# The folding product of the wide gates moved between the two tiles of the first ups block, the second activation ahead of the next rounded block

## What is computed

```python
def moe_swiglu(h, w_router, w_gu, w_down):
    logits = (h @ w_router).astype(jnp.float32)
    top_vals, top_idx = lax.top_k(logits, TOP_K)
    gates = jax.nn.softmax(top_vals, axis=-1)
    comb = jnp.sum(jax.nn.one_hot(top_idx, N_EXPERTS, dtype=jnp.float32) * gates[..., None],
                   axis=-2).astype(h.dtype)
    y = jnp.zeros_like(h)
    for e in range(N_EXPERTS):
        y = y + comb[..., e:e + 1] * swiglu(h, w_gu[e], w_down[e])
    return y
```

## Time and profile before

| | |
|---|---|
| median of 3 runs | 1629.64 us (1624.52 to 1630.21) |
| profiled execution, its own time | 1629.51 us |
| span from first to last instruction in it | 1627.7 us |
| PE, PEld, DVE, ACT busy | 1555.3, 1269.9, 1243.3, 1030.2 us |
| expert stage with the side expert | about 1000 to 1615 us of the span |
| wide chunks | 7, the folding product of the first at 1038.7 us, of the last at 1531.9 us |

### The profile page before, as it was taken

The page is one execution under the profiler, slowest core; times in us unless marked ns, Lnnn a source line. Parts: engine busy times, 40 slices in busy tenths (PEclk is TensorE's granted clock), DMA queues, the critical chain, the costliest instruction groups (busy, mean ns, idle before and its releaser), DMA issues.

```text
span 1627.7 us, 21967 instructions
## 1 busy us (share of the span) xinstructions
PE 1555.3 (96%) x7408; PEld 1269.9 (78%) x7409; DVE 1243.3 (76%) x1079; ACT 1030.2 (63%) x926; POOL 108.0 (7%) x87
## 2 busy tenths in 40 slices
PE   8999999999999898999999999999999999999997
PEld 6887778888789776677887887777777877787775
DVE  6744655544459878998888888887978797879788
ACT  5344444434345647887777768676768676867675
POOL 0000000000000005304003001000020002000000
PEclk9999999999989999999999999999999999999999
DMA  9663555555543037999998998999899989998994
GB/s 343 222 202 107 169 167 189 199 183 195 177 144 104 27 104 256 393 395 362 380 371 303 375 374 297 353 350 359 299 361 351 384 292 361 354 387 284 362 326 192
DMA packets 195751, 449.75 MB, mean 276 GB/s; under 512 B 8629, under 2 KB 17373, under 8 KB 195678
## 3 DMA queue, kind: packets, MB, share of 16 engines
q1 hardware_dynamic: 193340, 444.84, 76.0%
q10 hardware_dynamic: 2338, 3.88, 0.7%
HBM read 447.64 MB, written 1.05 MB: 276 GB/s over the span
## 4 chain that ended last, share of the span: by engine, by line
PE 69%; DVE 16%; issue 6%; DMA 4%; ACT 3%; DVEq 1%; ACTq 0%; POOL 0%; POOLq 0%; SPq 0%
PE bank L1717 14%; PE bank L1710 10%; PE bank L1711 10%; DVE wlo L985 9%; PE bank L1799 6%; DMA raw<-in_moe_w_down 4%; DVE y L1256 4%; PE bank L1788 3%; PE bank L1952 3%; PE bank L1740 3%; PE bank L1741 2%; PE bank L1747 2%; PE bank L1790 2%; PE bank L1791 2%; ACT whi L512 2%
## 5 line engine op out<-in xcount | busy, mean ns | idle before, releaser
L985 DVE TENSOR_TENSOR wlo<-raw,whi 128x2048 fp32r<-128x2048 f32 x422 | 956.2, 2290 | 238.8 <-ACT whi L512 235.8
L512 ACT ACTIVATE whi<-raw 128x2048 fp32r<-128x2048 f32 x422 | 804.1, 1917 | 395.1 <-PE bank L1717 240.4
L1717 PE MATMUL bank<-wlo,xx 128*128 128x512 f32 x1200 | 335.0, 401 | 29.6 <-DVE wlo L985 27.6
L1717 PEld LDWEIGHTS bank<-wlo,xx 128*128 128x128 f32 x1200 | 220.0, 189 | 107.3 <-DVE wlo L985 64.7
L1710 PE MATMUL bank<-whi,xx 128*128 128x512 f32 x648 | 255.0, 393 | 3.9 <-DVE xx L1464 2.3
L1711 PE MATMUL bank<-whi,xx 128*128 128x512 f32 x648 | 252.9, 390 | 0.0
L1708 PE MATMUL bank<-whi,xx 128*128 128x512 f32 x552 | 153.9, 401 | 0.4 <-ACT whi L512 0.2
L1710 PEld LDWEIGHTS bank<-whi,xx 128*128 128x128 f32 x648 | 121.9, 188 | 30.3 <-issue 3.5
L1711 PEld LDWEIGHTS bank<-whi,xx 128*128 128x128 f32 x648 | 122.0, 188 | 24.8
L1799 PE MATMUL bank<-wlo,hT 128*128 128x512 f32 x504 | 136.0, 392 | 1.3 <-DVE wlo L985 1.3
L1708 PEld LDWEIGHTS bank<-whi,xx 128*128 128x128 f32 x552 | 102.1, 190 | 23.2 <-issue 1.8
(11 more groups left out here) (294 smaller groups left out, 1696.7 us busy)
## 6 DMA issues: line engine op xcount, KB each, us to landing
raw<-in_moe_w_gu SPq DMA_DIRECT2D x224, 1024.0 KB, 7.7
raw<-in_moe_w_down SPq DMA_DIRECT2D x112, 1024.0 KB, 7.7
raw<-in_ffn_w_gu SPq DMA_DIRECT2D x28, 1024.0 KB, 5.1
raw<-in_ret_w_in SPq DMA_DIRECT2D x24, 1024.0 KB, 7.4
raw<-in_ffn_w_down SPq DMA_DIRECT2D x14, 1024.0 KB, 5.0
raw<-in_ret_w_out SPq DMA_DIRECT2D x8, 1024.0 KB, 5.0
raw<-in_conv_w_pw SPq DMA_DIRECT2D x16, 512.0 KB, 4.5
raw<-in_conv_w_pw SPq DMA_DIRECT2D x4, 1024.0 KB, 4.9
```

The costliest lines, as they stand in the source:

```text
L512: nc.scalar.activation(whi[base % SPLIT][:, :], raw[base % RAW][:, :], ACT.Copy).then_inc(hi_done, 1)
L985: nc.vector.tensor_tensor(wlo[base % SPLIT][:, :], raw[base % RAW][:, :], whi[base % SPLIT][:, :].bitcast(f32), ALU.subtract).then_inc(lo_ ...
L1717: last = nc.tensor.matmul(dst[:, :], both, wl, start=False, stop=closing and kc == DC - 1)
```

## The change

Two instructions change places on ACT, and one group on PE. On PE the wait for `gate1_out`, its branch and the folding product come ahead of the products of tile 2 in the first ups block, and so ahead of the `pe_done` of that block. On ACT the second silu comes ahead of hi(block). No instruction is added or taken away.

```diff
                 nc.scalar.activation(sgate[:, 1, :], bank[1][:, :], ACT.Copy).then_inc(gate1_out, 1)
                 nc.scalar.activation(sgate[:, 0, :], bank[0][:, :], ACT.Silu)
-                hi(block, six)
                 act.wait_ge(gate1_ps, count)
                 nc.scalar.activation(sgate[:, 1, :], bank[1][:, :], ACT.Silu).then_inc(silu_done, 2)
+                hi(block, six)
```

```diff
                     with pe.Else():
                         block_columns(base + 2 + half, bank[3], half, 3, HALF_FULL, six)
-                    block_columns(base + 2 + half, bank[2], half, 2, FULL, six).then_inc(pe_done, 1)
                     if half == 0:
                         pe.wait_ge(gate1_out, free)
                         with pe.If(need > 2):
                             nc.tensor.matmul(bank[1][:, :], ident, sgate[:, 1, :], start=True, stop=True).then_inc(gate1_ps, 1)
                         with pe.Else():
                             nc.tensor.matmul(bank[1][:, :], fold, sgate[:, 1, :], start=True, stop=True).then_inc(gate1_ps, 1)
+                    block_columns(base + 2 + half, bank[2], half, 2, FULL, six).then_inc(pe_done, 1)
```

## The result

The changed kernel takes 1633.6 us (median of 11 runs, 1631.62 to 1635.99). The kernel before, beside it, takes 1627.13 us (11 runs, 1622.22 to 1630.21). The ratio is 1.0048, with a 95% interval of 1.0039 to 1.0057: it is slower by 7.8 us, between 6.3 and 9.3. The ratio and its interval come from the single runs; it isn't the ratio of the two medians, which are 6.5 us (0.40%) apart.

The account below looks back on a forecast made before the run. The prediction took PE to bound the wide chunks: 1629.51 us plus seven stalls of 1.3 us gives 1638.6, and with the median 0.13 us above that execution 1638.7 us, 0.56% slower; range 1631 to 1643 us.

Parts of the forecast that it names:

- What bounds the chunk: In a wide chunk PE is the bound; a microsecond added to its queue delays everything behind it by a microsecond.
- ACT's half worth 0: Moving the second silu (0.58 us) on ACT brings 0, since it has some 3 us of room already.
- Rival (c): Faster: the second silu was on ACT's path, 7 x 0.58 = 4.1 us gained, 1625.5 us; chance 0.05.
- The stall: Before the folding product PE waits for ACT's copy, then branches: 1.29 us in each of seven wide chunks, 9.1 us.
- rival (a): The branch is covered and PE waits for the copy alone: 7 x 1.04 = 7.3 us, 1637.0 us; chance 0.15.
- The cost of the folding product: The folding product pushes PE's row of loads back about 0.87 us before and after alike: 0 for PE's end.
- The cover of lo(5): lo(5) comes 2.2 us later; of the 1.30 us idle before `hidden` 0.4 are left, no second loss.
- Whether it reaches the end: Each wide chunk is followed by a hole in the DMAs' work, so the stall counts in full, seven times.
- rival (b): Blocks loaded ahead swallow the delay after a wide chunk: all absorbed 1629.6 us, half 1634; chance 0.12.
- the holes in the DMAs' work: Expected in the profile after: the DMAs' idle stretches behind wide chunks are as long as before.
- rival (d): PE's new idle time lowers its clock, at least 1.1 us per wide chunk, 1646 us if all seven; chance 0.06.
- that line of the prediction's own: About 0.5%, 8.1 us, can be told from no change: above 1637.8 us is slower (0.57); same 0.38.

Follow-up runs that it names:

- act_only: Kernel before with only ACT's second silu moved ahead of hi(5), folding product left in place; ratio to before 1.0007, 1627.22 us beside 1625.69.
- fold_mid: Kernel before with the folding product in the middle of tile 2's products, ahead of pe_done; ratio to before 0.9999, 1625.64 us beside 1625.69.
- copy_first: Changed kernel with ACT's copy of bank 1 made ahead of hi(4) instead of behind it; ratio to before 1.0006, 1626.71 us beside 1625.69.
- no_branch: Changed kernel without the branch around the folding product, always multiplying by fold; ratio to before 1.0043 (1.0030 to 1.0057).
- pe_only: Changed kernel with ACT's two steps back in their old order, so only PE's move remains; ratio to before 1.0061, 1634.83 us beside 1625.69.
- copy_later: Changed kernel with ACT's first silu ahead of the copy of bank 1; ratio to before 1.0065 (1.0052 to 1.0078).

## Why the prediction was right or wrong

**What bounds the chunk: right.** Idle time on PE in a wide chunk went to the next chunk in full, by the short distances in the table above, and to the end in full as far as the ratios can tell. The three kernels without it (act_only, fold_mid, copy_first) are level with the kernel before, all four with it are slower.

**ACT's half worth 0: right**, by act_only within 0.17%. Rival (c) falls with it: the silu was not on the path.

**The stall: right in place and size.** Predicted were 1.29 us from the end of hi(4) and the copy plus the branch; the idle time is 1.34, of which 0.04 is the normal spacing of loads, so 1.30, and 1.43 in the first. The branch is part of it, 0.24 us by no_branch, so rival (a) with 1.04 us falls; the ratio alone would not have told, since 7.3 us lie inside its interval. The Trainium skill's figure in "Advanced Engine Details and Errata", "Control Flow Timing", 108 ns for a compare-and-branch, is too low for this branch: 202 to 212 ns, once 335. Other branches of PE's sequencer in the kernel before took 65 to 307 ns (line 2261), so one figure doesn't serve for all. The profile put the idle time down to "issue", not to ACT's line 831 as the prediction had it; only without the branch does it name ACT.

**The cost of the folding product: a term missed.** I took its 0.87 us as the same before and after. Behind an idle PE it is a little cheaper. Before, the second load behind it starts 1.08 us after its first (1038.51 to 1039.59); in copy_first, where it stands in the place of the change but behind other products, 1.09 us; after, 0.97 us (1202.24 to 1203.21):

```profile
1202.24 0.30 PEld L2323 LDWEIGHTS bank<-sgate,mats 128*128 128x128 f32 x2 [1.34 <-issue]
1202.78 0.19 PEld L1710 LDWEIGHTS bank<-whi,xb 128*128 128x128 f32 x1 [0.24 <-issue]
1203.21 0.19 PEld L1711 LDWEIGHTS bank<-whi,xb 128*128 128x128 f32 x1 [0.24 <-issue]
```

So a chunk lost 1.30 - 0.11 = 1.19 us, seven of them and the slower first branch 8.5 us, not 9.1. The short distances say the same, with 1.12 and 1.18 us, and not the 1.3 us that the prediction gave for the distance from chunk to chunk. Both measurements of the changed kernel hold that: 7.8 us (6.3 to 9.3) and 0.54% or 8.8 us (6.7 to 10.9).

**The cover of lo(5): right.** 0.4 us of idle time were to be left before `hidden`, and 0.39 are. act_only uses all of the 1.30.

**Whether it reaches the end: right; rival (b) falls.** In the two profiled executions of before and after the span grew by only 5.0 us, and between the first and the last copy by 5.1 (493.1 to 498.2) instead of six times 1.19, 7.1. That is no absorption: the missing 2 us lie in one distance, from the first copy to the second (88.3 us before, 87.5 after), and kernels without a stall were also faster there than the profiled execution of before (86.3 fold_mid, 87.0 copy_first, 87.4 act_only). The stretch 1075 to 1117 of the changed kernel, then of fold_mid (us, busy times, clock, DMA share, GB/s):

```profile
1075.00:1117.00 42.00, 40.56 (x196) 32.12 (x195) 40.89 (x23) 36.07 (x30) 0.00 (x0) 1.00 1.04 390
```

```profile
1075.00:1117.00 42.00, 40.59 (x195) 32.11 (x195) 40.90 (x24) 36.03 (x29) 0.00 (x0) 1.00 1.04 390
```

PE did 196 and 195 products in it where the execution of before did 186. It is the stretch in which the DMAs are full, and executions differ there; what makes them differ was not tried. One sign that the prediction named did not come: the holes in the DMAs' work were to be as long as before. In 20 us from a wide chunk on the DMA share is lower in the first (0.81 against 0.90) and the third (0.84 against 0.91), and higher in the second (0.75 against 0.70).

**The clock, rival (d): not seen.** In the ten microseconds from each folding product of the changed kernel the granted clock is 1.00, as it is with the longer stalls above.

**The time: inside the range partly by luck.** 1638.7 us was 5.1 too high. 2.5 of it is the base: the three runs shown had 1629.64, the eleven that they are part of have 1627.13. The missed term is 0.6 (0.8 less the 0.1 of the slower first branch), and the rest lies within what medians of such runs differ by. The range of the forecast and (a) with their own bounds began at 1636.9, so 1633.6 lies below it; it is inside 1631 to 1643 only because the range was widened for the half-absorbed (b), which did not happen, and for the differences between runs. The upper end, 1643, doesn't follow from the working either: 1641.1 and the same 5.7 would be 1646.8. The measured ratio lies just below the 0.5% that the forecast of 0.56% was just above. By that line of the prediction's own the outcome is "same", to which it gave 0.38 and not 0.57; yet the interval, 1.0039 to 1.0057, leaves no doubt that the kernel is slower.

## What to carry to other kernels

Before an instruction is moved up on a full engine, put its operand's time beside the time at which the engine gets there, and count what the producer has ahead of it (here a block of 1.92 us, released at the same moment). Work that a wait stands behind is free only as long as other work is queued in front; behind the short group of tile 3 there was none, and the branch behind the wait then counted too. If the operand can be made first on its own engine, the place doesn't matter, and what is left to gain is the length of the product.

## What the runs showed of the hardware that was not expected

A product in float32 behind an idle TensorE took 0.11 us less of the row of loads than one behind other products (0.97 against 1.08 us to the second load after it). Of the seven branches of the folding product the first took 335 ns in all five executions in which it stands right behind tile 3's products (the changed kernel twice, pe_only, copy_first, copy_later), and 217 at most where it stands later (before, act_only, fold_mid); what makes the difference was not tried. Two float32r products of 128 x 512 took 0.45 us where the float32 one took 0.87.
